# Full-width stationary tiles for the second and third term of the inverses' series (64 and 32 columns become 128)

## What is computed

```python
lmat = jnp.where(strict, jnp.einsum('nbhid,nbhjd->nbhij', k_beta, kc) * decay, 0.0)
tmat = lax.linalg.triangular_solve(eye + lmat, jnp.broadcast_to(eye, lmat.shape),
                                   left_side=True, lower=True, unit_diagonal=True)
u = jnp.einsum('nbhij,nbhjd->nbhid', tmat, v_beta)
w = jnp.einsum('nbhij,nbhjd->nbhid', tmat, k_beta * jnp.exp(gc)[..., None])
```

## Time and profile before

| | |
|---|---|
| Time of the kernel before, median of 3 runs | 1962.48 us (1962.11 to 1965.8) |
| Profiled execution, its own time | 1962.63 us |
| Span of the program in the profile | 1961.0 us |
| TensorE matmul busy | 1944.4 us, 99% of the span |
| TensorE weight load busy | 1545.3 us, 79% |
| VectorE / ScalarE / GpSimd busy | 1026.6 / 892.6 / 849.3 us |

### The profile page before, as it was taken

How to read it: one execution, slowest core, us unless ns; L and a number is a source line. 1 busy time by engine, 2 the same in 40 slices (tenths; PEclk the granted TensorE clock), 3 DMA queues, 4 the chain that set the end, 5 groups by cost and what they waited for, 6 DMA issues and landing times.

```text
span 1961.0 us, 24355 instructions
## 1 busy us (share of the span) xinstructions
PE 1944.4 (99%) x9372; PEld 1545.3 (79%) x9372; DVE 1026.6 (52%) x1873; ACT 892.6 (46%) x1375; POOL 849.3 (43%) x642
## 2 busy tenths in 40 slices
PE   9999999999999999999999999999999999999999
PEld 6878877877788778787877888677777888888887
DVE  5757755565745568756365557576443436101210
ACT  6455553334345555544343355686455344312321
POOL 4545432434355444422433455455222455444443
PEclk9999999999999999999999999999999999999999
DMA  5434542423534235522424545322111322222231
GB/s 201 127 117 134 136 136 76 154 85 118 189 123 145 98 118 153 158 91 76 153 75 145 183 152 161 127 84 86 55 51 48 122 104 97 97 97 97 97 113 70
DMA packets 94867, 227.74 MB, mean 116 GB/s; under 512 B 29880, under 2 KB 32952, under 8 KB 93440
## 3 DMA queue, kind: packets, MB, share of 16 engines
q1 hardware_dynamic: 89056, 223.03, 34.5%
q10 hardware_dynamic: 5696, 3.15, 0.6%
HBM read 194.01 MB, written 24.64 MB: 111 GB/s over the span
## 4 chain that ended last, share of the span: by engine, by line
PE 84%; DVE 8%; DMA 3%; ACT 3%; POOL 1%; SPq 1%; issue 1%; ACTq 0%; DVEq 0%
PE bank L439 83%; DVE ER L373 1%; DVE kv L373 1%; PE bank L443 1%; SPq L368 1%; DMA gt<-gates 1%; POOL wl L373 1%; ACT lt L425 1%; DMA X<-inverses 1%; DVE lt L383 1%; DVE scs L398 1%; DMA kv<-blocks 1%; DVE m8s L395 0%; ACT wh L428 0%; DVE tmp L373 0%
## 5 line engine op out<-in xcount | busy, mean ns | idle before, releaser
L373 POOL TENSOR_TENSOR wl<-st,wh 128x512 fp32r<-128x512 f32 x602 | 804.1, 1359 | 1034.5 <-ACT wh L428 1034.5
L439 PE MATMUL bank<-hh,wh 128*128 128x512 f32 x1616 | 651.9, 404 | 2.6 <-POOL hl L373 0.7
L439 PE MATMUL bank<-hh,wl 128*128 128x512 f32 x1616 | 629.8, 390 | 0.0
L439 PE MATMUL bank<-hl,wh 128*128 128x512 f32 x1616 | 629.4, 390 | 0.0
L428 ACT ACTIVATE wh<-st 128x1024 fp32r<-128x1024 f32 (+1 forms) x302 | 316.7, 1049 | 235.3 <-PE bank L439 188.2
L439 PEld LDWEIGHTS bank<-hh,wh 128*128 128x128 f32 x1616 | 303.3, 188 | 93.6 <-issue 26.1
L439 PEld LDWEIGHTS bank<-hl,wh 128*128 128x128 f32 x1616 | 303.6, 188 | 66.7 <-issue 7.0
L439 PEld LDWEIGHTS bank<-hh,wl 128*128 128x128 f32 x1616 | 303.4, 188 | 64.7
L373 DVE TENSOR_TENSOR xt<-xt,bank 128x512 f32<-128x512 f32 x40 | 27.4, 686 | 235.8 <-PE bank L439 235.8
L425 ACT ACTIVATE tmp<-bank 128x512 f32<-128x512 f32 x70 | 41.7, 596 | 157.3 <-PE bank L439 150.5
L439 PE MATMUL bank<-fh,wh 128*128 128x512 f32 x256 | 99.6, 389 | 0.0
(11 more groups left out here) (342 smaller groups left out, 2881.4 us busy)
## 6 DMA issues: line engine op xcount, KB each, us to landing
st<-units SPq DMA_DIRECT2D x300, 512.0 KB, 3.5
gates<-tmp SPq DMA_DIRECT2D x48, 256.0 KB, 2.9
gt<-gates SPq DMA_DIRECT2D x48, 256.0 KB, 3.7
pad<-tmp SPq DMA_DIRECT2D x32, 128.0 KB, 2.7
qk<-tmp SPq DMA_DIRECT2D x16, 256.0 KB, 4.3
x_scratch<-xt SPq DMA_DIRECT2D x2, 2048.0 KB, 8.6
xt<-x_scratch SPq DMA_DIRECT2D x2, 2048.0 KB, 8.0
ph<-phi SPq DMA_DIRECT2D x8, 512.0 KB, 4.5
```

The costliest lines, as they stand in the source:

```text
L373: return NOTHING if self.e is None else self.e.tensor_tensor(out, a, b, op)
L439: return NOTHING if self.e is None else self.e.matmul(out, lhsT, rhs, start=start, stop=stop, skip_group_check=share)
```

## The change

The stationary tile of the second and third term is `L.Y[e]`'s whole block of 128 columns and no longer its first 64 or 32. The product's output then has 128 rows of the PSUM bank and no longer 64 or 32. The moving columns `c` (the last 64 or 32 of each block), the semaphores, the order, and VectorE's update, which reads the same 64 or 32 rows as before, stay as they are. The rows of the bank beyond them are written and not read.

```diff
                     w = (128, 64, 32)[n]
                     for i in range(4):
                         c = slice(128 * i + 128 - w, 128 * i + 128)
-                        t = pe.mm(o[0:w, c], L.Y[e][:, 128 * i:128 * i + w], R[:, c], True, True)
+                        t = pe.mm(o[:, c], L.Y[e][:, sq4(i)], R[:, c], True, True)
                     t.then_inc(*sig("h_r", l, h, n))
```

## The result

The changed kernel takes 1967.99 us (median, 1966.53 to 1969.73). The kernel before takes 1963.78 us in the median of 11 runs (1962.11 to 1965.8), where the forecast started from 3 runs. The ratio is 1.0022, with a 95% interval of 1.0014 to 1.0031: slower, by 4.2 us where +4.1 us was forecast. The median of before is 1.3 us higher with the 11 runs, which is why the absolute number lies near the top of the wide range and just above the forecast's own range of 1965.6 to 1967.6 us.

A forecast was written before the change was run, and what follows sets the result against it. TensorE, busy 1944.4 of 1961.0 us, was taken to bound the kernel. Place changes of +0.09, +0.61 and +0.33 us, four times 1.03, gave +4.1 us on 1962.48: 1966.6 us, range 1964.5 to 1968.2 us.

The forecast's parts named there:

- the places: Three TensorE stretches with changed products, starting at projection matmuls: +1.03 us per head pair and layer, four times +4.1 us.
- a swallowed delay: Rival: TensorE's other waits shorten by some 1.5 us, kernel only +2.2 us, 1964.7 us; chance 0.09.
- A step with a full load: TensorE pass with 128 stationary columns loaded, start to next start: 0.112 us even with 64 or 32 moving columns.
- the template of 16 passes: Sixteen full-width fp32 passes between projection tiles on TensorE: 0.23 us entry, 0.112 us a pass, 0.33 us exit, 2.24 us.
- The two nearest rows: Trace rows with 128 stationary but 16 or 31 moving columns: 0.68 us for two passes, 0.111 us a step.
- hidden loads: Rival: full-width loads hide, steps stay 0.065 and 0.035 us, only switches go; -3.3 us, 1959.2 us; chance 0.06.
- loads and passes in turn: Rival: load and pass follow one another, steps 0.05 or 0.03 us longer; +9.2 us, 1971.7 us; chance 0.03.
- 8.5 us of longer loads, and 4.4 us given back by 28 changes of width: TensorE's 128 changed loads cost 8.5 us more; 28 column-width switches that go return 0.16 us each.
- the second place: TensorE stretch with second-term then third-term passes between projection matmuls, three switches: 1.63 to 2.24 us, +0.61 us.
- The waits of the earlier trace: TensorE waits for VectorE in the scan, a gate tile, a weight transfer, the inverses' transfer: each unchanged within 0.1 us.
- the first place: TensorE stretch with full-width and second-term passes between projection matmuls, two switches: 2.15 to 2.24 us, +0.09 us.
- the third place: TensorE stretch from a projection matmul through third-term passes to u and w, two switches: 1.01 to 1.34 us, +0.33 us.

The follow-up runs named there:

- the first four experiments: Against the kernel before: only third term full width, only second, both with 128 moving columns, 128 moving columns at old widths; +3.6, +2.2, +4.7, +7.7 us.
- full_move128: Kernel before with 128 stationary and 128 moving columns in the second and third term; 1967.58 us, ratio 1.0024.
- third_full: Kernel before with 128 stationary columns in the third term only, the second keeping 64; 1966.47 us, ratio 1.0021.
- narrow_move128: Kernel before with 64 and 32 stationary columns kept, but 128 moving columns in the second and third term; 1970.62 us, ratio 1.0042.
- first_in_step: Kernel before with only the first head pair's second terms, and third terms, side by side, one step more per layer; 1969.43 us against 1964.31.
- in_step: Kernel before with each head pair's second terms, and third terms, side by side, one step more per pair; 1965.21 us against 1963.85.

## Why the prediction was right, point by point

- TensorE bounds the kernel, and a delay there is passed on. Right: +4.1 us in the places and +4.2 us in the time. Over the first four experiments the places give +3.4, +1.3, +4.1 and +8.2 us (4 x (2.57 + 2.66 + 1.63 - 4.80), from 4.80 us per pair and layer today), the times +3.6, +2.2, +4.7 and +7.7 us, so the rival of a swallowed delay found no support.
- A step with a full load takes 0.112 us whatever it moves. Right: the template of 16 passes gave 2.24 us, and the places read 2.25, 2.25 and 1.34 us. The two nearest rows were good stand-ins; `full_move128` shows the step independent of the moved columns. The rivals of hidden loads and of loads and passes in turn are out by that and by `third_full`. The steps of today that the prediction worked out, 0.065 and 0.035 us, are a little high: they average over the longer first step of a group, and from the second pass on the starts lie 0.058 and 0.032 us apart in the trace of before. No term of the forecast rests on them, only the rival of hidden loads.
- 8.5 us of longer loads, and 4.4 us given back by 28 changes of width. Right in kind and size: `narrow_move128` gives 0.15 us a change, the middle of the second place 0.15 us (0.6 us over four), and 64 to 32 columns 0.14 us.
- VectorE's later updates stay hidden. Right: no wait for `ER` appears among PE's waits.
- The waits of the earlier trace rows would stay within 0.1 us. Wrong for two of the four, which moved by 0.5 us each. They vary between executions of one kernel: the changed kernel's two profiles have 1.6 and 2.2 us for the inverses' transfer, and 0.2 us and no such wait for the gate tile. They are noise on the result and not a part of it.

## What to carry to other kernels

Where loads of the stationary tile set TensorE's step, count their columns, and count how often the width of the column group changes: here the steps are 0.112, 0.058 and 0.032 us long with 128, 64 and 32 columns, so that eight of them saved 0.43 us with 64 columns and 0.64 us with 32, and each change of width took back 0.15 us. So narrow products pay most when they stand side by side. A lone group of eight between full-width work, with its two changes, barely pays with 64 columns (the first place is 2.15 us and would be 2.25) and saves 0.33 us with 32 (the third place is 1.01 us and would be 1.34). When products are moved to stand side by side, keep the number of steps of the woven orders: in `first_in_step` one step more per layer cost 6 us (+5.1 us where -0.9 was expected), more than the 4.2 us of all 28 changes of width together.

## What the runs showed of the hardware

The granted clock can fall behind a single wait of some two microseconds, and that costs 1.4 us on top of the wait itself. In `full_move128` PE waited 2.00 us for the inverses' transfer, a wait that lies ahead of the changed work and that took 0.74 us in the changed kernel's profile; then the clock stood at 0.50, the lower of its two levels (1.2 GHz), from 249 to 252 us. First the timeline, then the windows:

```profile
247.65 2.59 PE L439 MATMUL bank<-X,lT 128*128 128x128 f32 x15 [2.00 <-DMA X<-inverses]
```

```profile
249.00:252.00 3.00, 3.00 (x17) 2.90 (x17) 0.54 (x1) 2.58 (x6) 0.00 (x0) 0.50 1.06 399
252.00:256.00 4.00, 4.00 (x22) 2.98 (x21) 2.19 (x3) 1.54 (x3) 2.52 (x2) 0.99 0.19 47
```

The stretch from the first `W` to the scan takes 326.76 - 247.65 = 79.1 us in that layer and 898.75 - 821.07 = 77.7 us in the other one, which kept its clock: 1.4 us for the low clock. The waits of 1.70 us in `in_step` left the clock at 1.00 there, in both layers. The Trainium skill, TensorE: Matmul & The Clock Gate, Part 1, has the two levels, and says that an idle engine falls back to the lower; the trace agrees, with 1.92 and 2.00 us of idle time ahead of the falls shown here. How such a wait falls in one execution is, with the waits themselves, the likely reason why single times of one kernel spread over 4 us and more here. Of the 27 executions of the kernel before that were timed beside `in_step`, the four whose mean clock reads 0.999 have a median of 1967.3 us and the others one of 1963.3 us. That agrees with it; no row shows what made the clock fall in those four.
